# Down projections of a two-layer encoder: units of one row block by 1024 columns, three of eight pairs of row blocks by seven block products

## The reference

```
h   = RMSNorm(x);  qkv = h @ w_in                 # 2048 x 4352
x   = x + concat(A, B, C) @ w_out                 # three attention mixers, 2048 x 2048
x   = x + relu(RMSNorm(x) @ w_up)^2 @ w_down      # 2048 x 8192 and 8192 x 2048
```

## Time and profile before

| | |
|---|---|
| median of 3 runs (lowest, highest) | 2069.45 us (2069.18, 2069.55) |
| span of the profiled execution, first to last instruction | 2067.1 us |
| what lies around the span, against the median | 2.35 us |
| busy: PE, PEld, DVE, ACT, POOL | 100%, 84%, 61%, 48%, 9% of the span |
| mean rate of the DMAs, granted clock of TensorE | 192 GB/s, 0.9 or more of full speed in every slice |

### The profile page before, as it was taken

The page is one execution under the profiler, slowest core; times in us unless marked ns, Lnnn a source line. Parts: engine busy times, 40 slices in busy tenths (PEclk is TensorE's granted clock), DMA queues, the critical chain, the costliest instruction groups (busy, mean ns, idle before and its releaser), DMA issues.

```text
span 2067.1 us, 26774 instructions
## 1 busy us (share of the span) xinstructions
PE 2061.8 (100%) x10762; PEld 1733.5 (84%) x10762; DVE 1267.3 (61%) x1646; ACT 990.7 (48%) x1328; POOL 191.7 (9%) x196
## 2 busy tenths in 40 slices
PE   9999999999999999999999999999999999999999
PEld 7887788888888888888888877888888888888887
DVE  7767566655565556556677775665655655665664
ACT  6557644443443444344455586444434434434442
POOL 6253100000000000001023531000000000000000
PEclk9999999999999999999999999999999999999999
DMA  9477866666666666666665689666666666666663
GB/s 301 136 229 194 225 184 184 191 191 192 189 192 194 187 190 193 193 185 193 183 178 148 205 203 242 176 183 190 192 192 190 192 194 187 191 193 192 186 193 122
DMA packets 207451, 396.64 MB, mean 192 GB/s; under 512 B 13674, under 2 KB 22352, under 8 KB 207328
## 3 DMA queue, kind: packets, MB, share of 16 engines
q1 hardware_dynamic: 202640, 379.52, 61.9%
q0 software_dynamic: 4512, 15.33, 4.0%
q10 hardware_dynamic: 176, 0.09, 0.0%
HBM read 377.95 MB, written 2.12 MB: 184 GB/s over the span
## 4 chain that ended last, share of the span: by engine, by line
PE 99%; DMA 0%; SPq 0%; DVE 0%; issue 0%
PE psum L496 40%; PE psum L516 23%; PE psum L500 20%; PE psum L519 12%; PE psum L531 1%; PE psum L603 1%; PE psum L582 0%; PE psum L628 0%; PE psum L590 0%; PE psum L588 0%; DMA x<-in_x_dram 0%; PE psum L638 0%; PE psum L619 0%; PE psum L620 0%; PE psum L618 0%; PE psum L640 0%
## 5 line engine op out<-in xcount | busy, mean ns | idle before, releaser
L894 DVE TENSOR_TENSOR w_lo<-raw_ring,w_hi 128x1024 fp32r<-128x1024 f32 (+1 forms) x692 | 850.9, 1231 | 680.8 <-ACT w_hi L715 679.4
L715 ACT CAST w_hi<-raw_ring 128x1024 fp32r<-128x1024 f32 (+1 forms) x720 | 749.7, 1042 | 995.3 <-PE psum L500 604.1
L516 PE MATMUL psum<-xt,w_hi 128*128 128x512 f32 x2048 | 512.9, 392 | 0.0
L496 PE MATMUL psum<-w_hi,ht_hi 128*128 128x512 f32 x1280 | 501.8, 392 | 0.0
L496 PE MATMUL psum<-w_hi,ht_lo 128*128 128x512 f32 x1280 | 498.6, 390 | 0.0
L516 PEld LDWEIGHTS psum<-xt,w_hi 128*128 128x128 f32 x2048 | 368.8, 189 | 66.3
L500 PE MATMUL psum<-w_lo,ht_hi 128*128 128x512 f32 x1280 | 342.5, 389 | 0.0
L519 PEld LDWEIGHTS psum<-xt,w_lo 128*128 128x128 f32 x2048 | 279.4, 190 | 19.9
L519 PE MATMUL psum<-xt,w_lo 128*128 128x256 f32 x2048 | 285.6, 282 | 0.0
L500 PEld LDWEIGHTS psum<-w_lo,ht_hi 128*128 128x128 f32 x1280 | 240.3, 188 | 50.3
L496 PEld LDWEIGHTS psum<-w_hi,ht_hi 128*128 128x128 f32 x1280 | 240.4, 188 | 49.6 <-issue 1.0
(11 more groups left out here) (144 smaller groups left out, 968.2 us busy)
## 6 DMA issues: line engine op xcount, KB each, us to landing
raw_ring<-in_w_up_dram SPq DMA_DIRECT2D x256, 512.0 KB, 3.7
raw_ring<-in_w_down_dram SPq DMA_DIRECT2D x256, 512.0 KB, 3.7
raw_ring<-in_w_in_dram SPq DMA_DIRECT2D x128, 512.0 KB, 4.7
raw_ring<-in_w_out_dram SPq DMA_DIRECT2D x64, 512.0 KB, 4.8
w_lo<-raw_ring POOLq DMA_DIRECT2D x28, 512.0 KB, 5.8
raw_ring<-in_w_in_dram SPq DMA_DIRECT2D x16, 256.0 KB, 2.8
x<-in_x_dram SPq DMA_DIRECT2D x8, 256.0 KB, 7.5
out_dram<-x SPq DMA_DIRECT2D x3, 512.0 KB, 2.7
```

What stands on the lines that cost most here:

```text
L496: pe.matmul(bank[r][:, 0:cols], t[:, kt, r * P:(r + 1) * P], w_hi[:, slot, j, 0:cols], start=first and j == 0 and n == 0, stop=False, skip ...
L516: pe.matmul(bank[:, f, :], w_hi[:, w, j, f * P:(f + 1) * P], both, start=kt == 0, stop=False, skip_group_check=True)
L715: act.copy(w_hi[:, u % AHEAD, :, 0:cols], raw_ring[:, u % RAWS, :, 0:cols]).then_inc(hi_ready, 1)
L894: dve.tensor_tensor(w_lo[:, u % AHEAD, :, 0:cols], raw_ring[:, u % RAWS, :, 0:cols], w_hi[:, u % AHEAD, :, 0:cols].bitcast(F32), ALU.subtr ...
```

## The change

w_down's units in the three loop turns become one row block (128 rows) by 1024 columns, two column blocks of 512 side by side; two units, of row blocks four apart, are a pair. The 1024 output columns `d` = 0 or 1 take 16 units, eight pairs (`kp`). The eight blocks (two of rows of w, two of columns, two of tokens) of pairs 2, 4 and 6 are multiplied by Strassen's form in seven products instead of eight, 21 passes instead of 24. For it DVE makes sums of weight blocks (`t_raw`, four operations of 512 columns; one of them in place in the raw slot), ACT rounds three of them (`t_hi`), DVE subtracts (`t_lo`); and sums of token blocks are made once a turn (`s_raw`, `s_hi`, `s_lo`). The quarters of the result are summed in banks 4 to 7, the products that belong to several quarters in banks 0 to 3. At the end of each `d` DVE takes banks 0 to 3 into `totals` in SBUF (`take_totals`) and adds banks 4 to 7 to x (`take_quarters`); in the last down stage `add_totals` adds `totals` to x. As sums can no longer be scaled per row afterwards, the hidden values are scaled by 1/rms, spread along the tokens by two small matmuls a layer (`row_scales`, `row_scale`). The last down stage keeps its old units.

The core of the diff, TensorE's side:

```diff
+            def three(bank, a, w, first, hold=None):
+                (a_hi, a_lo), (b_hi, b_lo) = a, w
+                pe.matmul(bank, a_hi, b_hi, start=first, ...)
+                pe.matmul(bank, a_lo, b_hi, ...)
+                if hold is not None:
+                    hold()
+                return pe.matmul(bank, a_hi, b_lo, ...)
+            QUARTERS = [(1, 1), (0, 0), (0, 1), (1, 0)]      # banks 4, 5, 6, 7
+            def pair_steps(pl, s, d, m):
+                kp, half = m // 2, m % 2
...
+                if kp in SEVEN:
+                    if not half:
+                        seven_products(pl, s, d, kp, a, b, outs)
+                elif kp == KPS - 1:
+                    if not half:
+                        last_pair(pl, s, a, b)
+                else:
+                    pe.wait_ge(hi_ready, pl.unit(s + 1))
+                    kt = b if half else a
+                    for n, (r, h) in enumerate(QUARTERS):
+                        if d == 1 and m == 0:
+                            pe.wait_ge(pair_out, outs - PAIR_OUTS + 2 + n)
+                        for n, t in enumerate(h_tile(kt, r)):
+                            pe.matmul(quarter(r, h), t, w_hi[:, s % AHEAD, h, :], ...)
+                    unit_is_split(pl, s)
+                    for r, h in QUARTERS:
+                        mm = pe.matmul(quarter(r, h), h_tile(kt, r)[0], w_lo[:, s % AHEAD, h, :], ...)
+                    mm.then_inc(unit_done, 1)
+            def last_pair(pl, s, a, b):
+                for u in (s, s + 1):
+                    pe.wait_ge(hi_ready, pl.unit(u + 1))
+                    unit_is_split(pl, u)
+                for n, (r, h) in enumerate(QUARTERS):
+                    end = n == len(QUARTERS) - 1
+                    mm = three(quarter(r, h), h_tile(a, r), w_tile(s, h), False)
+                    if end:
+                        mm.then_inc(unit_done, 1)
+                    mm = three(quarter(r, h), h_tile(b, r), w_tile(s + 1, h), False)
+                    mm.then_inc(unit_done if end else pair_done, 1)
+            def seven_products(pl, s, d, kp, a, b, outs):
...
+                pe.wait_ge(hi_ready, pl.unit(s + 1))
+                three(psum[:, 0, :], h_tile(a, 0), w_tile(s, 0), first, lambda: unit_is_split(pl, s))
+                three(psum[:, 1, :], h_tile(a, 1), w_tile(s, 1), first).then_inc(unit_done, 1)
+                pe.wait_ge(hi_ready, pl.unit(s + 2))
+                three(quarter(0, 0), h_tile(b, 0), w_tile(s + 1, 0), False, lambda: unit_is_split(pl, s + 1))
+                three(quarter(0, 1), s_tile(2), w_tile(s + 1, 1), False)
+                pe.wait_ge(t_lo_ready, number + 1)
+                three(quarter(1, 0), h_tile(b, 1), t_tile(2), False)
+                three(psum[:, 2, :], s_tile(0), t_tile(1), first)
+                three(psum[:, 3, :], s_tile(1), t_tile(0), first).then_inc(unit_done, 1)
             def up_unit(pl, u, k, chunk):
+                    if kt == 0 and pl.i is not None and chunk == 17:
+                        pe.wait_ge(pair_out, pl.at(2 * LOOPS * PAIR_OUTS, PAIR_OUTS + 2 + f, 2 * PAIR_OUTS))
```

ACT's and DVE's side (`seven_at` tells whether a unit is the first, 0, or second, 1, of a pair of seven products):

```diff
             def split_hi(pl, u, cols=CW):
...
                 act.wait_ge(unit_done, pl.unit(u + 1))
+                if seven is not None and seven[0] == 0:
+                    act.wait_ge(t1_ready, seven[1] + 1)
                 act.copy(w_hi[:, u % AHEAD, :, 0:cols], ...).then_inc(hi_ready, 1)
+                if seven is not None and seven[0] == 1:
+                    act.wait_ge(t_raw_ready, seven[1] + 1)
+                    act.copy(t_hi[:, :, :], t_raw[:, :, :]).then_inc(t_hi_ready, 1)
             def split_lo(pl, u, cols=CW):
+                if after is not None and after[0] == 0:      # after = seven_at(pl, u + 1)
+                    first_sums(pl, u + 1)                     # two tensor_tensor of 512, then t1_ready
+                if seven is not None and seven[0] == 0:
+                    dve.wait_ge(t2_ready, seven[1] + 1)
+                    dve.tensor_tensor(t_raw[:, 2, :], raw_ring[:, (u + 1) % RAWS, 0, :], t_raw[:, 1, :], ALU.subtract).then_inc(t_raw_ready, 1)
                 dve.wait_ge(hi_ready, pl.unit(u + 1))
                 dve.tensor_tensor(w_lo[...], raw_ring[...], w_hi[...], ALU.subtract).then_inc(split_done, 1)
+                if after is not None and after[0] == 0:
+                    dve.tensor_tensor(t_raw[:, 1, :], ...).then_inc(t2_ready, 1)
+                if seven is not None and seven[0] == 1:
+                    dve.wait_ge(t_hi_ready, seven[1] + 1)
+                    dve.tensor_tensor(t_lo[:, :, :], t_raw[:, :, :], t_hi[:, :, :].bitcast(F32), ALU.subtract).then_inc(t_lo_ready, 1)
+            def take_totals(pl, d):                           # one operation of 2048 columns out of PSUM
+            def take_quarters(pl, s, d):                      # four of 512, each waits for its quarter and signals pair_out
             def mlp(pl, s, part, buf, c, k, n):
                 if s < UNITS - 1 and more:
                     split_lo(pl, s + AHEAD)
...
+                if part == "pair" and k == 2 * KPS - 2:
+                    dve.wait_ge(unit_done, pl.unit(s + AHEAD))
+                    take_totals(pl, c)
+                if part == "pair" and k == 2 * KPS - 1:
+                    take_quarters(pl, s, c)
+                if DOWN3 + 4 <= s < DOWN3 + 12:
+                    add_totals(pl, s - DOWN3 - 4)
...
+                    link(dve.scalar_tensor_tensor(mlp_t[q % 2], mlp_t[q % 2], 0.0, mlp_t[q % 2], ALU.max, ALU.mult))
+                    dve.tensor_tensor(v, v, row_scale[:, :]..., ALU.mult).then_inc(relu2, 1)
+                if made is not None:                          # pair steps 1 and 3 of d = 0, and steps 1 and 3 of each third up chunk
+                    token_sums(made[0])                       # step 1: four operations of up to 256 columns, two of them waited for
+                    token_lo(*made)                           # step 3: two, of up to 256 and 768 columns
```

More of the change, by code:

```diff
@@ L66 @@
 FIRST_LOADS = 4
-CHUNKS = NPROJ + 4 + 48
+CHUNKS = NPROJ + 4 + 4 + 4 * LOOPS + 8
 EVICTIONS = [(CHUNKS - 1) // 2, CHUNKS // 2]
-LOOP_EVICTIONS = 6
+LOOP_EVICTIONS = 2
+PAIR_UNITS = 32
+KPS = 8
+SEVEN = (2, 4, 6)
+BLOCKS = {b: [kp % 4 for kp in SEVEN if kp // 4 == b] for b in range(2)}
+SEVENS = LOOPS * 2 * len(SEVEN)
+PAIR_OUTS = 5
 SUMMED_UNITS = list(range(55, 83, 2))
@@ L191, in encoder, with over @@
         mlp_t = [head_in, head_sq]
+        with ExitStack() as mlp_only:
+            def over(name, shape, dt=F32):
+                return mlp_only.enter_context(nc.sbuf_tensor(name, shape, dt))
+            t_hi, t_lo = [over(f"t_{h}", [P, 3, CW], F32R) for h in ("hi", "lo")]
+            s_hi, s_lo = [over(f"s_{h}", [P, len(SEVEN), 3, P], F32R) for h in ("hi", "lo")]
+            t_raw = over("t_raw", [P, 3, CW])
+            row_scale = over("row_scale", [P, SEQ])
+            totals = over("totals", [P, 2, 4, CW])
         qk_t = [sb(f"qk_t{i}", [P, 4, SEQ]) for i in range(3)]
@@ L319, in mlp_steps @@
         def mlp_steps(first, kinds):
-            s, n = first, {UP0: 13, LOOP0: 17, DOWN3: 17 + 36}[first]
+            s, n = first, {UP0: 13, LOOP0: 17, DOWN3: 17 + 4 * LOOPS}[first]
             for kind in kinds:
-                if kind == "up":
+                if kind == "pair":
+                    for d in range(2):
+                        for m in range(2 * KPS):
+                            yield s, "pair", None, d, m, None
+                            s += 1
+                elif kind == "up":
                     for q in range(4):
@@ L344, in layer_steps @@
             for i in range(LOOPS):
-                for st in mlp_steps(LOOP0, ["down", "up"]):
+                for st in mlp_steps(LOOP0, ["pair", "up"]):
                     do_mlp(Place(l, i), *st)
@@ L510, in up_unit @@
                     pe.wait_ge(evicted[p], pl.evictions(chunk))
+                if k == 0 and pl.i is not None and chunk == 18:
+                    pe.wait_ge(pair_out, pl.at(2 * LOOPS * PAIR_OUTS, PAIR_OUTS + 1, 2 * PAIR_OUTS))
                 pe.wait_ge(hi_ready, pl.unit(u + 1))
@@ L521, in up_unit, with h_tile @@
                 mm.then_inc(unit_done, 1)
+            def three(bank, a, w, first, hold=None):
+                (a_hi, a_lo), (b_hi, b_lo) = a, w
+                pe.matmul(bank, a_hi, b_hi, start=first, stop=False, skip_group_check=True)
+                pe.matmul(bank, a_lo, b_hi, start=False, stop=False, skip_group_check=True)
+                if hold is not None:
+                    hold()
+                return pe.matmul(bank, a_hi, b_lo, start=False, stop=True, skip_group_check=True)
+            def h_tile(kt, r):
+                return [t[:, kt, r * P:(r + 1) * P] for t in ht]
@@ new lines, in seven_products, with s_tile, t_tile @@
+            def seven_products(pl, s, d, kp, a, b, outs):
+                i = SEVEN.index(kp)
+                first = i == 0
+                _, number = seven_at(pl, s)
```

(78 more changed lines are left out.)

108 lines of the change are left out of this document (91 added, 17 removed).

## The result

The changed kernel takes 2158.66 us (2158.36 to 2159.98) against 2069.31 us measured beside it: ratio 1.0432, 95% interval 1.0418 to 1.0447. The forecast was 2149, the range 2126 to 2176. The profiled execution's own time is 2158.36 us, its span 2156.6.

The account below looks back on a forecast made before the run. TensorE, busy through the whole span, was taken as the bound. On the profiled span 2067.1: −24.5 + 92.3 + 3 + 1 + 8 = +79.8, 2146.9; with 2.35 between span and median, 2149 us, range 2126 to 2176.

Parts of the forecast that it names:

- The passes saved: TensorE's down pairs: 36 seven-product pairs, 3 passes less each, 108 passes at 0.2267 us, saving 24.5 us.
- The ends of d: TensorE waits for DVE's totals and quarters, queued behind splits: 8.3 us after d = 0, 7.1 after d = 1; +92.3 us.
- DVE inside the pairs: DVE's added sums in pair stages make t_lo just late: 0.5 us a turn, 3 us in all, bounds 0 to 18.
- The small terms: Row-scale matmuls and the wait for row_scale's copy: 1 us for two layers (0.5 to 2); add_totals, scaling, loads cost nothing.
- The pace after a stand: TensorE runs at half pace for 2.3 us after each of twelve restarts: 8 us taken, ends 0 and 22.
- a clock below 1.00 for longer than 3 us behind a stand: Sign of being wrong: granted clock below 1.00 in windows behind TensorE's stands for longer than 3 us.
- the rival of the longer stretch: Each of 12 TensorE restarts runs at half clock for 4.6 us or more: 19 to 22 us, 2160 to 2163; 20%.
- DVE as bound: Rival: DVE's 77 us of work in 83.0 us of pair units becomes the bound, 2172 us; 15%.
- The faster side, hidden ends: Rival: DVE takes totals and quarters while the last pair runs, so 92.3 us fall to a few: 2049; 4%.
- Ends at a third of their cost: Rival: the ends of d cost about 28 us, for no reason seen: 2070 to 2080 us; 3%.

Follow-up runs that it names:

- eight_only: quarters_first with eight products in every pair, the seven-product branch, its sums, totals and add_totals taken out: 2073.44 us, ratio 1.0020 to the kernel before the change.
- two_of_eight: both_early with only two of eight pairs (kp 2 and 6) by seven products: 2065.30 us, ratio 0.9981 to the kernel before the change.
- both_early: Changed kernel with take_totals and take_quarters both moved ahead of the split at step 14: 2057.92 us, ratio 0.9944 to the kernel before the change.
- quarters_first: both_early with the two calls exchanged, quarters ahead of totals, the wait before them left out, pair_out counts renumbered: 2050.19 us, ratio 0.9908 to the kernel before.
- totals_early: Changed kernel with only take_totals moved ahead of the split at step 14, quarters left in place: 2135.69 us, ratio 1.0320 to the kernel before.
- signal_early: Changed kernel with last_pair's passes reordered so unit 14 is signalled after 12 passes, not 21; DVE's list untouched: 2136.86 us, ratio 1.0325 to the kernel before.

## Why the prediction was right, step by step

- *The whole.* 2158.66 lies inside the range, 9 us above the forecast of 2149 and 0.7 above the band given to it (2126 to 2158). The passes, the order and the length of the stands were right; the clock's share was too small, as below, and the bounds had room for it.
- *The passes saved.* 24.5 us forecast; eight_only and two_of_eight show it, by difference.
- *The ends of d.* Forecast from the 22nd pass's start: first quarter out at +8.38 and last at +10.21; in the timeline above that pass starts at 461.49, and the quarters are out at 469.10 + 0.68 = 469.78 and 469.10 + 2.47 = 471.57, so +8.29 and +10.08. (The prediction's own terms give +8.36 for the first, not +8.38.) After d = 1 the fourth was forecast at +8.36 and came at +8.29. Without the clock that is a delay of 8.1 and 7.0 us, 15.1 a turn where 15.4 were forecast. The order as cause is shown three ways: by both_early and quarters_first (moving the operations takes the stands away), totals_early (one operation, 2.2 us a stand) and signal_early (an earlier release, 2.0 us a stand). One reading of the rows was too wide: the 604 us that ACT waited for line 500 are 390 waits, and the down units are only 256, so that the line serves the projections too; nothing was added up from it.
- *DVE inside the pairs.* Forecast: `t_lo` of the second seven-product pair ends 24.05 us after the stage's first pass. It starts at 442.53, lasts 1.75, and the stage began at 420.23: 24.05. The wait is 1.9 us in six turns, where I took 3.
```profile
442.53 1.75 DVE L1094 TENSOR_TENSOR t_lo<-t_raw,t_hi 128x1536 fp32r<-128x1536 f32 x1
...
444.34 0.19 PEld L602 LDWEIGHTS psum<-t_hi,ht_hi 128*128 128x128 f32 x1 [0.55 <-DVE t_lo L1094]
```
- *The small terms.* The two row-scale matmuls stretch a unit to 3.16 us (2.79 before), the wait for `row_scale` another to 3.12: 0.7 us a layer, 1.4 in all where 1 was forecast.
- *The pace after a stand.* This term was mis-sized: 8 us forecast, and about 20 came. The spans differ by 89.5; 89.5 + 24.5 − 1.4 − 1.9 − 6 × 15.1 leaves 20. That is a remainder, and holds whatever else the sum left out. I took the length of the slow stretch from the start of the old trace, 2.3 us; in the windows above it is 3.0 to 6.0. The prediction had named a clock below 1.00 for longer than 3 us behind a stand as a sign of being wrong, and that sign came. The bounds, 0 to 22, held it, and the rival of the longer stretch (2160 to 2163) is nearer to the result than my middle: for this term the rival had the better size. In the first turn it cost 1.2 us after d = 0 (unit 17 begins 9.32 us late, of which 8.14 are the quarters) and 1.7 after d = 1 (8.70, of which 7.0). The Trainium skill (TensorE: Matmul & The Clock Gate, HAM oscillation) says that where the waits between bursts of matmuls send TensorE back to its half clock, this is paid anew at every burst. The trace agrees: the granted clock is 0.50 after the stands of both layers.
- *The rivals.* DVE as bound fell: waits of 1.9 us for `t_lo`, none for `w_lo`, and two_of_eight. The faster side, hidden ends, was right about its price (2049, against 2050.19 in quarters_first) and wrong about this kernel. Ends at a third of their cost fell too: they cost 6 × 15.1 = 90.6 us before the clock's share.

Not tried: removing the last `t_lo` wait and the 0.5 us at d = 1 in quarters_first, 1.9 + 3.2 = 5.1 us in all.

## What to carry to other kernels

When a stage begins to use every PSUM bank, its evictions come onto the path: look at what stands ahead of them in the evicting engine's list, and at which signal that waits for. An operation put behind a look-ahead step inherits that step's release, here a split for four units later that could not start before TensorE had finished; putting the evictions first took away 108 us without touching any arithmetic. Where a long stand can't be avoided, count the slow clock behind it too.

## What the runs showed of the hardware

TensorE's granted clock fell to 0.50 some 4 us into the first stand (mean 0.76 over the 7.6 us) and in the first turn of totals_early only 1.4 us after the restart from a stand of 3.6 us, so that the whole cost came on real work; in its second turn it fell 1.4 us before the restart from an equal stand. In the changed kernel it came back after 3.0 to 6.0 us of work at 0.43 us a pass. Extra matmuls in the stand moved part of that stretch out of the real work. The page's digits hardly show it: the mean granted clock over the span is 0.978.
